# Taking 64 instead of 128 value columns in the probability-times-value products of two attentions

## The reference, cut to what matters

```
# layer 1, neighbourhood attention: 8 heads, each query row sees 8 rows of 64 keys (512 keys) and 16 meta keys
p  = softmax(concat([q @ k_rows.T + bias, q @ k_meta.T]))
og = p_loc @ v_rows + p_meta @ v_meta          # per head: 64 value columns

# layer 2, windowed attention: 8 query heads share 2 key/value heads; blocks of 128 queries see 256 or 384 keys
probs = softmax(concat([scores, sink]))[..., :-1]
out   = probs @ v                              # per head: 64 value columns
```

## Time and profile before

| | |
|---|---|
| median of three runs | 2176.25 us |
| the profiled execution | 2176.4 us |
| its span, first to last instruction | 2174.6 us |
| mean granted TensorE clock | 0.921 |
| PE busy / PEld busy | 1855.4 us (85%) / 1576.2 us (72%) |
| DVE / ACT / POOL busy | 1036.7 us / 745.5 us / 91.1 us |
| the items of the first attention | about 216 to 324 us of the span |
| the items of the second attention | about 1091 to 1279 us |

### The profile page before, as it was taken

The page is one execution under the profiler, slowest core; times in us unless marked ns, Lnnn a source line. Parts: engine busy times, 40 slices in busy tenths (PEclk is TensorE's granted clock), DMA queues, the critical chain, the costliest instruction groups (busy, mean ns, idle before and its releaser), DMA issues. The chain is left out here.

```text
span 2174.6 us, 37914 instructions
## 1 busy us (share of the span) xinstructions
PE 1855.4 (85%) x16676; PEld 1576.2 (72%) x16676; DVE 1036.7 (48%) x1467; ACT 745.5 (34%) x1211; POOL 91.1 (4%) x84
## 2 busy tenths in 40 slices
PE   5999994765799999954999968888858899999988
PEld 4998773665698998834777747777747678887866
DVE  3212663654653453553645336566565453433445
ACT  3221445122443342422433334444324342332323
POOL 2000000003000000030000000000000200000020
PEclk7999995777799999976999989999988999999999
DMA  5520001000322222203212110000005222222221
GB/s 157 138 78 1 1 1 60 1 20 1 116 79 96 97 89 86 98 0 112 78 58 93 72 49 3 3 4 3 9 12 213 77 80 95 97 97 97 97 78 58
DMA packets 24233, 141.66 MB, mean 65 GB/s; under 512 B 4203, under 2 KB 4459, under 8 KB 8972
## 3 DMA queue, kind: packets, MB, share of 16 engines
q1 hardware_dynamic: 21228, 130.76, 16.8%
q0 software_dynamic: 2560, 7.87, 1.5%
q10 hardware_dynamic: 288, 0.71, 0.1%
HBM read 133.03 MB, written 6.29 MB: 64 GB/s over the span
## 5 line engine op out<-in xcount | busy, mean ns | idle before, releaser
L237 PE MATMUL f_bank<-f_u_hi,f_w_hi 128*128 128x258 f32 x704 | 201.4, 286 | 16.1 <-DVE f_w_lo L225 14.5
L238 PE MATMUL f_bank<-f_u_hi,f_w_lo 128*128 128x258 f32 x704 | 200.8, 285 | 0.0
L239 PE MATMUL f_bank<-f_u_lo,f_w_hi 128*128 128x258 f32 x704 | 199.3, 283 | 0.0
L237 PE MATMUL g_bank<-g_u_hi,g_w_hi 128*128 128x512 f32 x384 | 152.9, 398 | 17.0 <-DVE g_u_lo L2360 13.6
L238 PE MATMUL g_bank<-g_u_hi,g_w_lo 128*128 128x512 f32 x384 | 151.2, 394 | 0.0
L239 PE MATMUL g_bank<-g_u_lo,g_w_hi 128*128 128x512 f32 x384 | 151.1, 393 | 0.0
L237 PE MATMUL g_bank<-g_y_hi,g_w_hi 128*128 128x512 f32 x336 | 133.1, 396 | 18.4 <-DVE g_w_lo L225 11.6
L237 PEld LDWEIGHTS f_bank<-f_u_hi,f_w_hi 128*128 128x128 f32 x704 | 133.6, 190 | 17.7 <-DVE f_w_lo L225 15.2
L212 ACT ACTIVATE g_w_hi<-g_w_raw 128x2048 fp32r<-128x2048 f32 x45 | 85.9, 1909 | 174.2 <-PE g_bank L239 171.9
L239 PEld LDWEIGHTS f_bank<-f_u_lo,f_w_hi 128*128 128x128 f32 x704 | 134.6, 191 | 0.0
L238 PEld LDWEIGHTS f_bank<-f_u_hi,f_w_lo 128*128 128x128 f32 x704 | 134.0, 190 | 0.0
(11 more groups left out here) (409 smaller groups left out, 4334.1 us busy)
## 6 DMA issues: line engine op xcount, KB each, us to landing
g_w_raw<-in_w_ff SPq DMA_DIRECT2D x32, 1024.0 KB, 4.8
f_w_raw<-in_w_ffn_in SPq DMA_DIRECT2D x22, 1024.0 KB, 4.8
a_w_raw<-in_w_in SPq DMA_DIRECT2D x18, 1024.0 KB, 4.8
m_w_raw<-in_w_in SPq DMA_DIRECT2D x13, 1024.0 KB, 4.9
f_w_raw<-in_w_ffn_out SPq DMA_DIRECT2D x12, 1024.0 KB, 4.8
m_w_raw<-in_w_o SPq DMA_DIRECT2D x4, 1024.0 KB, 4.8
gate_pre<-rw_t POOLq DMA_DIRECT2D x16, 256.0 KB, 2.3
g_w_raw<-in_w_up SPq DMA_DIRECT2D x4, 1024.0 KB, 8.7
```

The source lines that it names most:

```text
L237: nc.tensor.matmul(out, w_hi, u_hi, start=start, stop=False)
L238: nc.tensor.matmul(out, w_lo, u_hi, start=False, stop=False)
L239: return nc.tensor.matmul(out, w_hi, u_lo, start=False, stop=stop)
```

## The change: what it does

The value matmuls stream only the 64 columns of the head in question and write 64 columns of PSUM; `read_o` reads these 64. The number of instructions on every engine, their order and all semaphores stay. The weights that are loaded (128 columns of probabilities) stay.

```diff
 def read_o(i):                                  # first attention
     dst = proj[:, hh // 2, META + P * t + 64 * (hh % 2):META + P * t + 64 * (hh % 2) + 64]
-    nc.scalar.activation(dst, bank[:, b, P + 64 * (hh % 2):P + 64 * (hh % 2) + 64], ACT.Copy,
+    nc.scalar.activation(dst, bank[:, b, P:P + 64], ACT.Copy,
                          scale=rden[:, i:i + 1]).then_inc(o_read, 1)
...
 def values(i):                                  # first attention
-    cols = slice(P * (hh // 2), P * (hh // 2) + P)
+    cols = slice(64 * hh, 64 * hh + 64)
     for k in range(4):
-        nc.tensor.matmul(bank[:, b, P:2 * P], pt[:, i % 2, k * P:k * P + P], vg[:, k, cols],
+        nc.tensor.matmul(bank[:, b, P:P + 64], pt[:, i % 2, k * P:k * P + P], vg[:, k, cols],
                          start=k == 0, stop=False)
-    nc.tensor.matmul(bank[:, b, P:2 * P], ptm[:, i % 2, :], vg[0:META, 4, cols],
+    nc.tensor.matmul(bank[:, b, P:P + 64], ptm[:, i % 2, :], vg[0:META, 4, cols],
                      start=False, stop=True).then_inc(o_done, 1)
...
 def values(i):                                  # second attention
+    at = 640 + HD * (i % 8 // 4)
     for b, kb in enumerate(ks):
         c = c0 + P * b
-        last = nc.tensor.matmul(bank[:, 2 + i % 2, 0:P], pt[:, i % 2, c:c + P], tok[:, kb, 640:768],
+        last = nc.tensor.matmul(bank[:, 2 + i % 2, 0:HD], pt[:, i % 2, c:c + P], tok[:, kb, at:at + HD],
                                 start=b == 0, stop=b == len(ks) - 1)
...
 def read_o(i):                                  # second attention
-    at = 64 * (hh // 4)
-    nc.scalar.activation(tok[:, n, hh * HD:hh * HD + HD], bank[:, 2 + i % 2, at:at + HD], ACT.Copy,
+    nc.scalar.activation(tok[:, n, hh * HD:hh * HD + HD], bank[:, 2 + i % 2, 0:HD], ACT.Copy,
                          scale=rden[:, i:i + 1]).then_inc(o_read, 1)
```

## The result

The changed kernel took 2252.37 us (median of 4 runs, 2247.97 to 2254.11), the kernel before 2177.6 us beside it. The ratio is 1.0343, with a 95% interval of 1.0322 to 1.0365. The forecast was 2172.0 with a range of 2166 to 2177: wrong in sign.

What follows compares the result with a forecast made beforehand. TensorE's own sequence of passes was taken to bound both attentions. Savings of 31 x 0.128 = 4.0 us in the first and 0.4 in the second, 4.4 in all, took 2176.4 to 2172.0 us; range 2166 to 2177.

Steps and rivals of the forecast that it cites:

- What bounds the stretches: Both attention stretches: as long as TensorE's own sequence of passes, busy 90.40 of 90.40 us and 173.03 of 173.40.
- A pass can't get under its load: Passes in a row: the 128-column weight load stays at 0.108 us though the stream falls to 0.053.
- eight passes at 0.108: First attention, L664: eight passes per item at 0.108 instead of 0.111 us, saving 0.02 us per item.
- second attention: Second attention's value passes: 0.002 to 0.003 us saved for each of 160 passes, 0.4 us in all.
- The two tails: First attention: last streams of L664 and L666, each ahead of a change of rows, save 0.053 us each per item.
- The rate of 0.107 for 128 columns: Value passes: a 128-column stream takes 0.107 us, taken from half-speed streaming at 2.4 GHz.
- The slack: First attention: the softmax chain has 0.43 us of slack per item, of which the change takes 0.13.
- the last item: First attention: no saving in one of 32 items, as TensorE waits for ScalarE before its transposes.
- The clock: Rival, chance 0.06: shorter streams drop the first attention's clock to 0.50 for half the stretch, 30 us more, 2202 us.
- Transposes count as work: Against the falling clock: a stretch with 14 transposes and no other matmul was followed by a rise from 0.50 to 1.00.

Runs made afterwards that it cites:

- e5: The changed kernel with three full 512-column matmuls (result unread) before the transposes of item 0 in the first attention; 2166.28 us, ratio 0.9953.
- e2: The kernel before, with the change applied to the second attention only; 2177.08 us, ratio 0.9999.
- e3: The kernel before, first attention only: three of four value matmuls keep 128 columns, the last and the meta one take 64; 2174.94 us, ratio 0.9986.
- e4: The changed kernel with ten full 512-column matmuls (result unread) before the transposes of item 0 in the first attention; 2176.69 us, ratio 1.0001.
- e8: The changed kernel with 24 transposes of 128x128 (result unread) before the transposes of item 0 in the first attention; 2169.12 us, ratio 0.9962.
- e9: e5's kernel with a pause: ScalarE copies a weight slot four times before item 16's exponential; 2216.03 us.
- e6: The changed kernel, but values of items 0 and 1 of the first attention keep 128 columns, nothing added; 2172.39 us, ratio 0.9985.
- e10: The kernel before with a pause: ScalarE copies a weight slot four times before item 16's exponential; 2187.61 us.
- e11: The kernel before, first attention only: two of four value matmuls keep 128 columns, the other two and the meta one take 64; 2252.75 us.

## Why the prediction was wrong, by its own steps

- *What bounds the stretches* was right: TensorE's own sequence, at either clock. One reading beside it was not: TensorE's 85% is 1.8 times VectorE's 48%, not twice and more.
- *A pass can't get under its load* was right, and a row of loads does not even go to 0.108: with 64 columns it stays at 0.111 (0.97 us for eight in e5). The term "eight passes at 0.108" (0.02 us per item) is zero. So is "second attention" (0.4 us) as far as e2's loads show; its ratio of 0.9999 (0.999 to 1.0008) could not tell 0.4 us from nothing.
- *The two tails* were right: 0.05 and 0.06 us per item in e5, 3.3 us forecast for them in all, 2.8 measured in e3. The rate of 0.107 for 128 columns, which the prediction took without seeing it by itself, can be seen in the kernel before: the second pass of L643 (512 columns) starts at 259.10 and the next pass at 259.53, and a quarter of these 0.43 us is 0.107.
- *The slack* was right: no wait of TensorE for L468 in e5's steady items, and L468's reads only follow. So was the last item: from the transposes of the one before it (L654's load at 317.05) to its own (319.91) it is 2.86 us before, and 314.25 - 311.39 = 2.86 in e5, so nothing is saved there.
- *The clock* is the step that failed. The sum of 4.4 us left it out, and it cost 75.6 us in the first attention. It stood among the rivals at 0.06 and 2202 us; it came true at 2252. Two things in it were wrong. First, the question: I asked whether the remaining work holds the full clock, and it does (e4, e5, e8). But the stretch begins with a fall, so the question was whether the remaining work raises the clock from 0.50, and there it fails: the changed kernel and e9 stay down, e6 and e10 come up with 128 columns. The earlier trace rows answered for transposes alone, not for this mix. Second, the price: I let the clock be low for half of the stretch at 5.2 us per item. Once it stays down it stays for all, at 5.71 us per item: the 5.5 from the earlier trace rows ended at full clock (up from 226.1), and an item of 128 columns wholly at 0.50 took 5.93 in e10.
- *Transposes count as work* was right (e8). The rule of the Trainium skill that I had set against it ("TensorE: Matmul & The Clock Gate", "Part 4: PE-mode transpose") says that the full clock does not engage for transposes; the transposes timed there are 16-bit. For the 32-bit ones here e8's trace and the earlier trace rows show the opposite.

Why does the narrow item stay down? The runs show the difference in what ran, not the reason in the chip. At half clock the loads slow down too, to 0.214 apart. By the 0.85 us for 512 columns, a stream of 128 fills that time (0.213) and one of 64 half of it, while PE is "busy" in the rows either way. That the chip goes by this is not shown, and the cause stays open there.

## What to carry to other kernels

Where the granted clock falls once inside a stretch, ask whether what comes after it can raise the clock, and not only whether it can hold it: before streams are shortened, look for falls in the clock of that stretch and at what ran just ahead of each rise. Halving the 128 columns streamed against 128 columns of weights saved nothing here but the last stream ahead of a change of rows (0.05 us each); the loads, 0.111 apart, set the pace. If such a cut is made, fill the idle time ahead of the stretch (2.8 us of unread matmuls or transposes gave 2166 to 2169 us here, a part of it from the RWKV stage, where the bare change gave 2252). A single later pause undoes it (e9). Keeping 128 columns in the first two items gave 2172 without filling (e6), and was not tried with a pause.

## What was not expected of the hardware

- The same sequence of items ran at 1.00 for 90 us (e5) or at 0.50 for 160 us (the changed kernel). The kernels differ only in 2.8 us of filling ahead of it.
- No state in between was seen: with six wide value passes per item the clock came up after 6.8 us (e3), with four it was still down at 390 us, some 170 us after the fall (e11).
- The distance of loads of 128 columns was 0.111 us with 128 and with 64 columns streamed, though L666's two loads stand about 0.108 apart (by rounding within 0.005).
